# First attention: transposes one unit later, probabilities of five units in the memory of four, the product with z a step behind its sums

## What is computed

```python
s_s = einsum(q, k_sel) - slopes * distance          # all 8 blocks are selected, so it is causal attention
p_s = _masked_softmax(s_s, causal);  o_s = einsum(p_s, v_sel)
s_w = einsum(q, k_win) - slopes * distance          # window of 512: causal attention again, other k and v
p_w = _masked_softmax(s_w, causal);  o_w = einsum(p_w, v_win)
o = gate_c * o_c + gate_s * o_s + gate_w * o_w      # o_c from 31 compressed keys, made before this stage
y = (o * silu(z)) @ w_out
```

## Time and profile before

| | before |
|---|---|
| median of 3 runs | 1909.52 us (1909.1 to 1912.31) |
| the profiled execution | 1908.04 us |
| its span, first to last instruction | 1906.2 us |
| PE busy | 1802.1 us, 95% |
| DVE / ACT / POOL busy | 970.5 / 852.4 / 170.3 us |
| mean granted clock of PE | 0.983 |
| the attention: first exponential to the first matmul of w_o0 | 208.5 to 397.4 us |

### The profile page before, as it was taken

The page is one execution under the profiler, slowest core; times in us unless marked ns, Lnnn a source line. Parts: engine busy times, 40 slices in busy tenths (PEclk is TensorE's granted clock), DMA queues, the critical chain, the costliest instruction groups (busy, mean ns, idle before and its releaser), DMA issues.

```text
span 1906.2 us, 24071 instructions
## 1 busy us (share of the span) xinstructions
PE 1802.1 (95%) x9772; PEld 1449.9 (76%) x9772; DVE 970.5 (51%) x1640; ACT 852.4 (45%) x1437; POOL 170.3 (9%) x293
## 2 busy tenths in 40 slices
PE   6899998899999999999999999999899899999996
PEld 4677786679988877865877778877687678888885
DVE  7878556854854373344345554355534534434223
ACT  6445666645363243334355553365523433323222
POOL 2000226510000000000000000022200001111000
PEclk9899999999999999999999999999999899999998
DMA  4553441044423323211322222211232122332331
GB/s 135 169 197 119 128 111 45 1 137 179 145 96 104 104 88 112 92 44 45 109 86 78 78 78 89 83 65 56 67 100 89 67 78 89 100 99 87 101 100 55
DMA packets 60318, 181.28 MB, mean 95 GB/s; under 512 B 7008, under 2 KB 18080, under 8 KB 57776
## 3 DMA queue, kind: packets, MB, share of 16 engines
q1 hardware_dynamic: 60208, 179.75, 29.1%
HBM read 165.57 MB, written 16.25 MB: 95 GB/s over the span
## 4 chain that ended last, share of the span: by engine, by line
PE 73%; DVE 13%; ACT 9%; POOL 3%; issue 2%; DMA 0%; SPq 0%; DVEq 0%; ACTq 0%
PE bank L901 17%; PE bank L903 17%; PE bank L902 17%; DVE wlo L1951 2%; PE bank L964 2%; PE bank L966 2%; PE bank L965 2%; POOL Ps L2719 2%; PE bank L1127 1%; ACT L1401 1%; PE bank L1106 1%; ACT Ps L1849 1%; ACT whi L1396 1%; PE bank L921 1%; PE bank L922 1%
## 5 line engine op out<-in xcount | busy, mean ns | idle before, releaser
L1951 DVE TENSOR_TENSOR wlo<-wraw,whi 128x1024 fp32r<-128x1024 f32 (+1 forms) x262 | 316.3, 1209 | 324.0 <-ACT whi L1396 322.7
L901 PE MATMUL bank<-Hh,whi 128*128 128x512 f32 (+2 forms) x1104 | 445.6, 404 | 16.3 <-DVE wlo L1951 16.3
L903 PE MATMUL bank<-Hh,wlo 128*128 128x512 f32 (+2 forms) x1104 | 433.8, 393 | 0.0
L902 PE MATMUL bank<-Hl,whi 128*128 128x512 f32 (+2 forms) x1104 | 433.5, 393 | 0.0
L1396 ACT ACTIVATE whi<-wraw 128x1024 fp32r<-128x1024 f32 (+1 forms) x262 | 271.5, 1040 | 293.2 <-PE bank L903 225.6
L901 PEld LDWEIGHTS bank<-Hh,whi 128*128 128x128 f32 (+2 forms) x1104 | 208.2, 189 | 74.7 <-DVE wlo L1951 18.6
L903 PEld LDWEIGHTS bank<-Hh,wlo 128*128 128x128 f32 (+2 forms) x1104 | 207.9, 188 | 46.4
L902 PEld LDWEIGHTS bank<-Hl,whi 128*128 128x128 f32 (+2 forms) x1104 | 208.2, 189 | 45.3 <-issue 2.2
L1401 ACT ACT_TABLE_LOAD x97 | 124.5, 1283 | 2.8 <-DVE epst L1966 1.1
L901 PE MATMUL bank<-Bh,whi 128*128 128x512 f32 x256 | 102.2, 399 | 2.2 <-DVE Bl L2494 2.2
L903 PE MATMUL bank<-Bh,wlo 128*128 128x512 f32 x256 | 100.9, 394 | 0.0
(11 more groups left out here) (370 smaller groups left out, 3037.2 us busy)
## 6 DMA issues: line engine op xcount, KB each, us to landing
wraw<-in_w_o SPq DMA_DIRECT2D x24, 512.0 KB, 3.4
wraw<-in_w_bgate SPq DMA_DIRECT2D x24, 512.0 KB, 3.4
wraw<-in_w_branch SPq DMA_DIRECT2D x24, 512.0 KB, 3.4
wraw<-in_w_fg SPq DMA_DIRECT2D x22, 512.0 KB, 3.4
wraw<-in_w_fu SPq DMA_DIRECT2D x22, 512.0 KB, 3.4
wraw<-in_w_glu SPq DMA_DIRECT2D x16, 512.0 KB, 3.4
wraw<-in_w_fd SPq DMA_DIRECT2D x16, 512.0 KB, 3.5
scratch_CA<-CA SPq DMA_DIRECT2D x4, 1152.0 KB, 6.5
```

Of the source, the lines that this page charges most:

```text
L901: pe.matmul(o, wh[:, cols], hi(k), start=k == 0, stop=False)
L902: pe.matmul(o, wh[:, cols], lo(k), start=False, stop=False)
L903: m = pe.matmul(o, wl[:, cols], hi(k), start=False, stop=k == K - 1)
L1951: dve.tensor_tensor(c.wlo[q][:, 0:n], c.raw[i % RR][:, 0:n], c.whi[q][:, 0:n].bitcast(F32), S_).then_inc(*up(DID, ("wlo", i)))
```

## The change

The transposes of a unit come a step later (`nc(i-4)` in step i), the sums of a pair too (`nd(i-7)`, in odd steps), and the product with z and its split are a step of their own (`no`, `stage_e`), one step after the sums, two steps later than before. For that, P has to hold five units. They lie in the same 16 KB: each unit has only the bytes that its length needs, at a place from a table, and `na(u)` waits for the last unit that had a byte of that place, which is five or six units before. `x_again` comes a step later.

```diff
+        def stage_e(u):
+            t, a, j = units[u]
             if j == 3:
+                self.step("no", u)
                 self.bank.give(("o", t))
                 self.step("split_g0", t)
...
-            if 3 <= i <= n + 2:
-                stage_c(i - 3)
-            if i % 2 == 0 and i >= 6:
-                stage_d(i - 6)
-            if i == AWAY + 4:
+            if 4 <= i <= n + 3:
+                stage_c(i - 4)
+            if i % 2 and i >= 7:
+                stage_d(i - 7)
+            if i % 2 == 0 and i >= 8:
+                stage_e(i - 8)
+            if i == AWAY + 5:
                 self.step("x_again")
...
-        if u >= 4:
-            on.wait_ge(*at("p", u - 4, len(plan.nsa_parts(plan.units[u - 4][2])) - 1))
-            on.wait_ge(*at("pn", u - 4, 0))
-            on.wait_ge(*at("pn", u - 4, 1))
+        v = c.P_before(u)
+        if v is not None:
+            on.wait_ge(*at("p", v, len(plan.nsa_parts(plan.units[v][2])) - 1))
+            on.wait_ge(*at("pn", v, 0))
+            on.wait_ge(*at("pn", v, 1))
...
-        return (self.Pb if u < AWAY else self.Pl)[u % 4]
+        return (self.Pb if u < AWAY else self.Pl)[u // 8 % 2, u % 8]
+    P_AT = (14, 15, 8, 0, 2, 5, 12, 8)
+    def P_span(self, u):
+        kb = u % 8 // 2 + 1
+        at = self.P_AT[u % 8]
+        return (at, at + kb) if u // 8 % 2 == 0 else (16 - at - kb, 16 - at)
```

More of the change, by code:

```diff
@@ L455, in attention @@
         n = len(units)
-        for i in range(n + 6):
+        for i in range(n + 7):
             if i < n:
@@ L2103, in nc, with no @@
                 *up(DID, ("pT", u, 0), ("freed", ("p", u, 0))))
-    def nd(u):
-        t, _, j = plan.units[u]
-        if j == 3:
-            on.wait_ge(*at("pv", u, 1))
-            on.wait_ge(*at("z0", t))
-            dve.tensor_tensor(c.zs[:, t, :], c.zs[:, t, :], bank(("o", t)), M).then_inc(
-                *up(DID, ("o", t), ("freed", ("o", t))))
+    def no(u):
+        t = plan.units[u][0]
+        on.wait_ge(*at("pv", u, 1))
+        on.wait_ge(*at("z0", t))
+        dve.tensor_tensor(c.zs[:, t, :], c.zs[:, t, :], bank(("o", t)), M).then_inc(
+            *up(DID, ("o", t), ("freed", ("o", t))))
     big = float(np.float32(1.5 * 2 ** 23))
@@ L2604, in vector @@
                     norm0=norm0, ev=ev, gate_t=gate_t, cmp_out=cmp_out, soft_in=soft_in, soft_out=soft_out,
-                    na=na, prep_r_wide=prep_r_wide, nb=nb, nc=nc, nd=nd, prep=prep, prep_b=prep_b, prep_ca=prep_ca, prep_w=prep_w,
+                    na=na, prep_r_wide=prep_r_wide, nb=nb, nc=nc, no=no, prep=prep, prep_b=prep_b, prep_ca=prep_ca, prep_w=prep_w,
                     store_k=store_k, split_g0=split_g0, split_h1=split_h1, s5_in=s5_in, rsS=rsS, rows=rows, states=states,
@@ L2779, in x_again @@
     def x_again():
-        for u in range(AWAY - 4, AWAY):
+        for u in range(AWAY - 5, AWAY):
             on.wait_ge(*at("p", u, len(plan.nsa_parts(plan.units[u][2])) - 1))
@@ L2978, in first_mixer @@
         self.Rh = h.take("Rh", [128, 4, 2, 8, 64])
-        self.Pl = [h.take(f"Pl{i}", [128, 2, 512])[:, :, :] for i in range(4)]
+        self.Pl = self.places("Pl", h.at)
         x = Region(self.nc, self.X_at)
@@ L2983, in first_mixer @@
         self.tB = [x.take(f"tB{i}", [128, 8, 16]) for i in range(2)]
-        x = Region(self.nc, self.X_at)
-        self.Pb = [x.take(f"Pb{i}", [128, 2, 512])[:, :, :] for i in range(4)]
+        self.Pb = self.places("Pb", self.X_at)
         self.WT = [self.lent.take(f"WT{i}", [128, 8, 8, 16]) for i in range(2)]
@@ L3073, in P, with places, P_before @@
     def P(self, u):
-        return (self.Pb if u < AWAY else self.Pl)[u % 4]
+        return (self.Pb if u < AWAY else self.Pl)[u // 8 % 2, u % 8]
[4 more added lines that the diff above has]
+        return (at, at + kb) if u // 8 % 2 == 0 else (16 - at - kb, 16 - at)
+    def places(self, name, at):
+        place = {}
+        for n in range(16):
+            lo, hi = self.P_span(n)
+            place[n // 8, n % 8] = self.nc.alloc_sbuf_tensor_at(
+                f"{name}{n}", [128, 2, (hi - lo) * 128], F32, offset=at + lo * 1024)[:, :, :]
+        return place
+    def P_before(self, u):
+        lo, hi = self.P_span(u)
+        for v in range(u - 1, -1 if u < AWAY else AWAY - 1, -1):
+            vlo, vhi = self.P_span(v)
+            if vlo < hi and lo < vhi:
+                assert u - v >= 5
+                return v
+        return None
     def banked(self, key):
```

## The result

| | before | changed |
|---|---|---|
| median of 20 runs each | 1909.31 us (1906.83 to 1912.63) | 1903.71 us (1898.78 to 1909.79) |
| ratio, 95% interval | | 0.9973 [0.9964, 0.9982] |
| profiled execution | 1908.04 us, span 1906.2 | 1906.97 us, span 1905.2 |
| first exponential of the attention | 205.20 | 204.51 |
| w_o0 starts | 397.41 | 393.45 |

The change makes the kernel 5.6 us faster between the medians, against 4.8 forecast. The profiled execution of the changed kernel is one of its slower ones, so its span shows only 1.0 us; within the attention it shows 3.27 us. That is PE's idle time: of the attention PE is idle 16.3 us before and 13.0 after, and it is busy 175.9 us in both.

A forecast was written before the change was run, and what follows sets the result against it. PE was taken as 95% busy, with only its 15.3 us of attention idle time winnable. Terms 1.9 + 0.6 + 2.4 + 0.9 - 1.0 = 4.8 us took 1909.5 to 1904.7 us, range 1901.5 to 1909.3.

The forecast's parts named there:

- Term 1: POOL's busy stretch from 302.4 us: starts earlier, as the product comes after pair 28's normalization; 1.9 us gained (0 to 2.6).
- Term 2: End of POOL's busy stretch, to 326.3 us: the product's 2.61 us wait for sums goes; 0.6 us gained (0 to 1.4).
- Term 3: Wide stretch, 326.3 to 370.99 us: DVE's waits of 0.20 and 1.00 us per tile go; 2.4 us gained (0 to 2.4).
- Term 4: 371 to 388 us, PE the limit: shorter way from unit 52's transposes to unit 60's scores; 0.9 us gained (0 to 1.5).
- Term 5: The tail: last in-loop product delays unit 63's scores on DVE, w_o0 later; -1.0 us (-2.6 to 0).
- nothing is to be won: 207 to 288 us: the z projection fills PE, busy 79.95 of 81 us, so no gain there.
- the price of a missing cover: First 81 us of the attention: the added step is hidden behind the z projection; without that, a 2.18 us stall.
- a gap near 2 us stays: Sign, wide stretch: a PE gap near 2 us remains ahead of units 44 and 52, where it was 2.44.
- a PE with fewer gaps would keep 2.4 GHz: 302.4 to 326.3 us: sums 1.3 us shorter without half clock; counted as nothing because POOL is behind anyway.
- more is won: Rival, 12%: DVE carries the path from 302 to 390 us and the tail costs nothing; 7.9 us gained, 1901.6.
- the buffer changes nothing: Rival, 31%: where POOL and DVE are the limit nothing is won; 1.4 us left, 1908.1, no change that can be told.
- The slower case: Rival, 9%: in the tail, step 62's product delays the last scores and PE falls to half clock; 3.0 us slower, 1912.5.

The follow-up runs named there:

- again: The changed kernel profiled and timed a second time with no edit; ratio to the kernel before 0.9963.
- fill: The changed kernel with PE's longest gaps filled by repeated matmuls and transposes that are thrown away; ratio to the kernel before 0.9962.
- shift_only: The changed kernel with the product with z put back in the step of its sums, transposes still a unit later; ratio to the kernel before 0.9960.
- product_10: The changed kernel with every product a pair of steps later still (i-10 instead of i-8 in step i); 1895.53 us, ratio to the kernel before 0.9924.
- nowide_before: The kernel before with DVE's 18 wide instructions replaced by nine short writes; one run, 187.91 us from first exponential to w_o0.

## Why the prediction was right, and which of its terms were not

The time was 1.0 us below the forecast and inside the range, the sign was right, and so was the mechanism: a buffer whose use ends where DVE is the limit, though the largest term had another cause than I had given. The single terms were less good than their sum. Gained between marks (before less kernel; the times of the columns above, and unit 60's first scores on PE at 174.24 before, 170.31 in the changed kernel, 168.74 in again and 167.75 in fill, from the first exponential):

| term, marks | forecast (ends) | changed | again | fill |
|---|---|---|---|---|
| 1, up to pair 32 | 1.9 (0, 2.6) | 3.5 | 3.5 | 3.5 |
| 2, pair 32 to 38 | 0.6 (0, 1.4) | 0.9 | 1.1 | 0.7 |
| 3, pair 38 to 54 | 2.4 (0, 2.4) | 2.0 | 0.6 | 2.0 |
| 4, pair 54 to unit 60's scores | 0.9 (0, 1.5) | -2.4 | 0.3 | 0.3 |
| 5, from unit 60's scores to w_o0 | -1.0 (-2.6, 0) | -0.7 | -0.6 | -0.6 |
| sum | 4.8 | 3.3 | 4.9 | 5.9 |

A mark needs the same work ahead of it in both orders. Terms 4 and 5 meet at unit 60's scores, as in the prediction, and not at POOL's start on pair 60: the sums of pair 54, 1.97 us on PE, stood ahead of unit 61's scores and now stand behind them, so pair 60 comes 1.8 us sooner after unit 60's scores (6.5 us in place of 8.3) without anything being won. POOL's starts on pairs 38 and 54 may carry a shift of the same kind, alike for both, so term 3 is free of it, and terms 2 and 4 are less sure.

**Term 1 was too small, and for a reason that was wrong.** I took its 2.6 us from the product's leaving its place ahead of the normalization of pair 28. shift_only leaves the product there, with the sums, and pair 32 starts at the same 108.3. The gain is that of the scores that lie a unit ahead. Part of it is there already when the z projection ends (78.28 against 76.92), in the stretch where "nothing is to be won": up to that mark PE is idle 0.9 us before and 0.4 after. The rest of the 1.36 us is no gain, for of 90 transposes ahead of the mark four now stand behind it. The larger part is the 2.18 us gap at 292.62, which I named only as the price of a missing cover; in the changed kernel waits of 0.61 and 0.88 us stand at 286.78 and 288.81 in place of its 0.58 and 2.18, and PE's idle time between 288 and 302.4 falls from 2.66 to 0.81 us.

**Term 2 held**, with 0.7 to 1.1 for 0.6: the product's wait of 2.61 us is gone. What is late next is POOL on pair 34, as was said: PE waits 2.05 us for it.

**Term 3 held in kind.** The waits of 1.00 us are gone, 0.30 stay, and a tile takes 19.7 us in place of 20.7, so 2.0 of 2.4. again has 0.6, with its half clock in this stretch. That a gap near 2 us stays was right (1.12 + 0.87 and 1.78 + 0.84), and the runs without the wide instructions show why. What I had not seen is that the gap would be split, its second part behind ACT's copies. On ACT these copies stand behind the exponentials of the tile's last scores. The product stands ahead of those scores on DVE; but product_10, where it doesn't, still has a wait of 0.87 us for ACT in each tile, so that the product causes it is shown for the tail alone.

**Term 4 was too large at full clock and lost where the half clock fell.** At full clock it is 0.3 us for 0.9, within its ends. In the changed kernel's trace it is a loss of 2.4 us, below its end of 0: the half clock, which I counted at nothing, "because POOL is behind in any case there". That holds for the place of the earlier trace rows, up to 326 us: pairs 32 to 38 start within 0.2 us of fill's. It does not hold from 366 to 372 us, where PE is the limit. I had argued from the kernel before, whose clock stayed at 1.00 through both gaps of 2.44 us; the changed kernel has 0.92 in that stretch with shorter but double gaps. The Trainium skill ("TensorE: Matmul & The Clock Gate", "What's actually happening") has the half clock as the default that activity releases, and I used it to say that a PE with fewer gaps would keep 2.4 GHz. The trace disagrees with that use of it: PE's idle time between 326.3 and 370.99 fell from 7.20 to 4.99 us and the half clock there rose from none to 7 us of the 44.69.

**Term 5 held, step by step.** Unit 60's scores start at 374.83, and behind them:

```profile
374.83 0.44 PE L1102 MATMUL bank<-kh,qs 128*128 128x384 f32 x1
...
379.68 0.69 DVE L2072 CUSTOM_DVE_ANT_0 Pl<-bank,bias 128x512 f32<-128x512 f32 x1 [1.44 <-PE bank L1103]
...
384.10 0.68 DVE L2072 CUSTOM_DVE_ANT_0 Pl<-bank,bias 128x512 f32<-128x512 f32 x1
```

Unit 62's minimum starts 4.9 us behind them (4.7 was said), unit 63's 9.3 (9.2), and w_o0 18.6 (18.9, where it was 18.0 before). PE idles 2.06 us there, ahead of sums and not of unit 62's transposes. The product is the price, as was said: the tail edit, which moves only this product, brings w_o0 to 16.8 us behind unit 60's scores.

So the sum came out near by some luck. At full clock term 1 is 1.6 us too small, terms 3 and 4 are 0.4 and 0.6 too large, and terms 2 and 5 together 0.5 too low, which leaves 1.1 us more than forecast; the half clock, priced at nothing, takes 1.0 to 2.6 us of it back. In the rival "more is won" the first three terms, 6.4 us, are what was measured (6.2 in fill), with the cause of the first wrong; its 1.5 us in term 4 and its free tail did not come. The rival "the buffer changes nothing" falls with the 4.3 us at pair 28. The slower case had its mechanism, product and half clock together, and the half clock did come, but at 366 us and not in the last sums, which took 3.28 us as before. None fell between 390 us and w_o0.

The time outside the attention is not constant either. From w_o0 to the end of the span the profile has 1508.8 us before and 1511.7 after, with the same instructions; the other traces have 1507 to 1512.6. That is as large as the effect, and the reason why the spans of two profiles differ by 1.0 us where the medians differ by 5.6.

## What to carry to other kernels

Deepening a buffer by one unit pays where the consumer's waits are waits for order, and here the first such waits stood ahead of the stretch that looked limited. A step that is moved on an engine that runs in order must go behind the instruction that others wait for, not merely later: here one step later than the sums was worth nothing and three steps later 0.4%. When two orders are compared at a mark, ask what work has changed sides of the mark. Before a term is priced at one clock, read whether PE is the limit there, and take the profile of a kernel with short gaps twice.

## What the hardware did that I had not expected

**The half clock falls behind some short gaps and not behind others.** It fell after gaps of 2.05 us and of 1.78 + 0.84 us in one execution and at 344 us, after 1.77 us, in another of the same kernel, while the kernel before stayed at 2.4 GHz through two gaps of 2.44 us. The same gap can do either. At the place where the changed kernel's clock fell after 2.05 us, again and product_10 kept 2.4 GHz:

```profile
318.82 0.80 PE L1112 MATMUL bank<-ident,Pl 128*128 128x128 f32 x4 [2.05 <-POOL Pl L2701]
...
319.64 0.80 PE L1112 MATMUL bank<-ident,Pl 128*128 128x128 f32 x4 [2.06 <-POOL Pl L2701]
```

(the first row is of again, the second of product_10). So the length of the gap alone does not decide it; what does, no run here tells. Per microsecond at 1.2 GHz the changed kernel's attention grew by next to nothing where POOL was behind, by 0.15 us in DVE's stretch and by 0.4 where PE was the limit. The Trainium skill ("TensorE: Matmul & The Clock Gate", "HAM oscillation — how this bites in real kernels") describes a clock that falls again in the waits between bursts, of 3 to 5 us there; these traces agree that it falls again, and here it did so behind waits of 2 us and less. The page's "Terms" put the penalty at the throttled time times the share of pulses withheld, which is half; only the stretch where PE is the limit comes near that, with 0.4, and for the whole attention the measurement decides, with less than 0.2.

**POOL is slower beside DVE's wide instructions.** Groups of POOL's normalization, mean ns of one after the busy time, between 326.3 and 370.99 us, before:

```profile
L2695 POOL TENSOR_SCALAR Pl<-Pl,stp 128x512 f32<-128x512 f32 x8 | 7.1, 910 | 3.3 <-DVE stp L1919 3.3
...
L2695 POOL TENSOR_SCALAR Pl<-Pl,stp 128x128 f32<-128x128 f32 x8 | 3.7, 482 | 0.2
```

and in nowide_before, the same stretch:

```profile
L2692 POOL TENSOR_SCALAR Pl<-Pl,stp 128x512 f32<-128x512 f32 x12 | 8.1, 695 | 6.3 <-DVE stp L1919 6.3
...
L2692 POOL TENSOR_SCALAR Pl<-Pl,stp 128x128 f32<-128x128 f32 x8 | 2.8, 376 | 1.1 <-DVE stp L1919 1.1
```

Without the wide instructions one of 128x512 takes 695 ns in place of 910, and one of 128x128 takes 376 in place of 482. The wide ones, which take both of their inputs from SBUF (tR<-Rh, Rh<-tR), thus cost DVE's time and POOL's too. The Trainium skill ("SBUF — State Buffer", "Who interferes with whom") says that a DVE instruction with two inputs in SBUF contends with a GpSimd instruction that reads SBUF; the trace agrees, with 0.1 to 0.2 us more for each.
